# Delta rule: products of constants, read by nobody, at the places in levels three to five of the inverse where TensorE waits

## The reference, cut to what matters

```python
def gated_delta_chunked(q, k, v, log_a, beta, s0):
    ...
    g = jnp.cumsum(log_a, axis=-1)
    decay = jnp.exp(jnp.where(causal, g[..., :, None] - g[..., None, :], -jnp.inf))
    kk = jnp.einsum('bhncd,bhnsd->bhncs', k, k)
    lmat = jnp.where(strict, beta[..., :, None] * decay * kk, 0.0)
    rhs = jnp.concatenate([beta[..., None] * v, (beta * jnp.exp(g))[..., None] * k], axis=-1)
    sol = lax.linalg.triangular_solve(jnp.eye(GDN_CHUNK, dtype=f32) + lmat, rhs,
                                      left_side=True, lower=True, unit_diagonal=True)
    ...
    def step(s, inp):
        u0_c, w_c, aqk_c, qg_c, kg_c, gl_c = inp
        u = u0_c - w_c @ s
        o = qg_c @ s + aqk_c @ u
        s = gl_c[..., None, None] * s + jnp.swapaxes(kg_c, -1, -2) @ u
        return s, o
```

## Time and profile before

| what | value |
|---|---|
| median of 3 runs | 3951.13 us |
| the runs | 3950.55 to 3952.97 us |
| the profiled execution, its own time | 3950.24 us |
| its span, first to last instruction | 3948.4 us |
| outside the span | 1.8 us |
| mean granted TensorE clock | 0.994 of full speed |
| busy: PE, PEld, DVE, ACT, POOL | 97%, 73%, 56%, 19%, 18% |
| the delta rule's four heads | about 484 to 732 us |

### The profile page before, as it was taken

One profiled execution on the slowest core, in us unless ns is written; L12 is line 12 of the kernel. 1 busy time (PEld: TensorE's weight loads), 2 busy tenths in 40 slices (PEclk: granted clock), 3 DMA queues, 4 the chain that ended last, 5 costly groups with the idle time before them and its releaser, 6 DMA issues.

```text
span 3948.4 us, 48505 instructions
## 1 busy us (share of the span) xinstructions
PE 3838.0 (97%) x18602; PEld 2875.3 (73%) x18602; DVE 2228.2 (56%) x3856; ACT 742.5 (19%) x1402; POOL 721.9 (18%) x570
## 2 busy tenths in 40 slices
PE   7999988999999999999999999999999999999998
PEld 3455567565555556688888877888789898778886
DVE  4255676354446313326565765564788888556546
ACT  2144455221110013431100000000311111100002
POOL 0048853100000000000000002120244343121200
PEclk9999999999999999999999999999999999999999
DMA  5244400231211121112322322232222222122321
GB/s 192 89 167 149 139 2 1 71 90 53 63 53 59 59 75 43 33 60 80 85 83 88 85 77 92 87 102 86 77 70 70 70 73 64 54 85 85 101 86 64
DMA packets 381407, 312.13 MB, mean 79 GB/s; under 512 B 9552, under 2 KB 349904, under 8 KB 381136
## 3 DMA queue, kind: packets, MB, share of 16 engines
q1 hardware_dynamic: 381264, 310.16, 25.2%
HBM read 308.03 MB, written 2.10 MB: 79 GB/s over the span
## 4 chain that ended last, share of the span: by engine, by line
PE 87%; POOL 5%; DVE 3%; ACT 2%; issue 1%; DMA 1%; POOLq 0%; SPq 0%; DVEq 0%; ACTq 0%
PE ps_lin L967 18%; PE ps_lin L867 10%; PE ps_d L967 9%; PE ps_lin L1742 6%; PE ps_d L867 5%; PE ps_c L967 4%; PE ps_lin L750 4%; PE ps_lin L767 3%; PE ps_d L750 3%; PE ps_lin L813 3%; PE ps_lin L1158 3%; PE ps_c L867 3%; POOL arena L3506 2%; PE ps_d L1531 2%; POOL arena L3503 2%; PE ps_c L750 2%
## 5 line engine op out<-in xcount | busy, mean ns | idle before, releaser
L3475 POOL TENSOR_TENSOR rstd<-square 128x512 f32<-128x512 f32 (+2 forms) x12 | 15.1, 1260 | 1543.3 <-ACT square L1920 1543.3
L967 PE MATMUL ps_lin<-arena,ring 128*128 128x256 f32 (+1 forms) x800 | 217.2, 424 | 1.1 <-DVE arena L2597 1.1
L867 PE MATMUL ps_lin<-arena,ring 128*128 128x256 f32 (+1 forms) x864 | 214.1, 401 | 0.0
L967 PEld LDWEIGHTS ps_lin<-arena,ring 128*128 128x128 f32 x800 | 151.8, 190 | 60.9 <-issue 2.9
L867 PEld LDWEIGHTS ps_lin<-arena,ring 128*128 128x128 f32 x864 | 164.2, 190 | 41.1
L967 PE MATMUL ps_lin<-hid_in,arena 128*128 128x256 f32 x832 | 188.6, 380 | 3.6 <-DVE arena L2624 3.6
L3478 POOL TENSOR_TENSOR rstd<-rstd,square 128x512 f32<-128x512 f32 (+2 forms) x58 | 75.4, 1300 | 631.2 <-ACT square L1920 630.3
L967 PE MATMUL ps_d<-arena,mixed 128*128 128x384 f32 (+1 forms) x672 | 187.7, 432 | 0.0
L967 PE MATMUL ps_lin<-hid_in,mixed 128*128 128x384 f32 (+1 forms) x672 | 187.7, 432 | 0.0
L2621 DVE TENSOR_TENSOR arena<-ring 128x1024 f32<-128x1024 f32 x84 | 102.9, 1225 | 146.3 <-PE ps_d L867 136.0
L967 PEld LDWEIGHTS ps_lin<-hid_in,arena 128*128 128x128 f32 x832 | 157.7, 190 | 27.7 <-DVE arena L2624 5.6
(11 more groups left out here) (545 smaller groups left out, 8132.8 us busy)
## 6 DMA issues: line engine op xcount, KB each, us to landing
ring<-in_ffn_w_in SPq DMA_DIRECT2D x88, 512.0 KB, 4.6
resid<-in_ada_w SPq DMA_DIRECT2D x20, 2048.0 KB, 7.9
ring<-in_mlp_w_up SPq DMA_DIRECT2D x64, 512.0 KB, 4.5
ring<-in_mlp_w_down SPq DMA_DIRECT2D x64, 512.0 KB, 4.4
ring<-in_attn_w_qkv SPq DMA_DIRECT2D x64, 512.0 KB, 4.8
ring<-in_ffn_w_out SPq DMA_DIRECT2D x32, 512.0 KB, 4.1
ring<-in_even_w_in SPq DMA_DIRECT2D x28, 512.0 KB, 5.0
ring<-in_sc_w_in SPq DMA_DIRECT2D x24, 512.0 KB, 4.5
```

What stands on the lines that cost most here:

```text
L867: last = mm(prod[i - 1], lhs[:, j, :], rhs(p), start=(g == j == 0), stop=(g == G - 1 and j == np_ - 1))
L967: last = mm(out, lhs[:, j, :], rhs[:, j, :], start=(j == 0), stop=(j == 3))
```

## The change: what it does

A helper `keep_busy(count)` issues `count` matmuls of `ident` with the 256 columns of `upto` into columns 768 to 1023 of `ps_c`. They wait for no semaphore, release none, and nothing reads what they write. For heads 0 to 2 (n is not None) and levels 3, 4 and 5 they stand: in level 3, five ahead of the third group of products, two ahead of the third group of updates and seven behind it; in level 4, two ahead of the third group of updates; in level 5, seven behind the products and two ahead of the third group of updates. That is 25 matmuls a head, 75 in all. No other engine's instructions change.

```diff
+                def keep_busy(count):
+
+                    for _ in range(count):
+                        mm(psc[:, T:1024], ident, flat(m["upto"]), start=True, stop=True)
+
                 for e in range(1, LEVELS):
+                    busy = n is not None and 2 < e < LAST
                     if e == LAST:
...
                     for g in range(3):
+                        if busy and e == 3 and g == 2:
+                            keep_busy(5)
                         products(e, g)
+                    if busy and e == 5:
+                        keep_busy(7)
                     for g in range(3):
+                        if busy and g == 2:
+                            keep_busy(2)
                         updates(e, g)
+                    if busy and e == 3:
+                        keep_busy(7)
```

## The result

The kernel with the change takes 3958.08 us (median of 22 runs, 3956.02 to 3960.2), the one before 3950.37 us (22 runs, 3945.5 to 3952.97): 7.7 us more, a ratio of 1.0021 with a 95% interval of 1.0015 to 1.0027, which is 5.9 to 10.7 us. The profiled execution took 3958.11 us, its span is 3956.3 us.

The account below looks back on a forecast made before the run. TensorE, busy 97% of the span, was taken to bound the kernel: 16.2 us of added delay less 6.6 us from the clock gave +9.6 us on 3950.24 us, so 3959.9 us, with a range of 3952 to 3967 us.

Parts of the forecast that it names:

- The price of a matmul and of the turn: TensorE, heads 0 to 2: 0.429 us a new matmul, another 0.33 us for a group between quarter-array matmuls.
- Rival 1: Going between quarter and full array costs nothing: +4.6 us, 3954.8 us; chance 22%.
- The delays: Heads 0, 1 and 2, levels 3 to 5: added delay of 6.6, 4.8 and 4.8 us, together 16.2 us.
- The chain argument: Levels 3 to 5: each group less its idle time, remainders adding up on TensorE; 4.35 us at head 1's level 5 updates.
- One reading in the chain: Head 1, level 5: the transposes that ended the gap were taken to come 3.17 us late.
- What the clock gives back: Half-clock stretches avoided from level 5 on: 5.55 us in head 1, 1.00 us in head 2, together 6.6 us.
- The signs: Clock 1.00 from 505 to 720 us, 150 L1443 records, head 0's scan at 541.5 us, head 1's 64.8 us later.
- Rival 2: New matmuls don't hold the clock in these levels: +16.2 us at least, 3966.4 to 3970.3 us; chance 17%.
- The clock rule of the Trainium skill: Mid-kernel drops only behind pauses longer than any of levels 3 to 5; the change would be all cost, +16.2 us.
- Rival 3: Level 5 of each head: faster if avoided falls exceed 16.2 us; over 0.2% faster needs 24 us; chance 6%.
- Rival 4: Later stages shift against the clock's falls, up to 3.5 us either way, heads as forecast; chance 10%.

Follow-up runs that it names:

- the twos: The change without its nine groups of two matmuls ahead of third updates: 3953.91 us, ratio 1.0008 to the kernel before.
- level 5's groups: The change with its new matmuls in level 5 alone, 27 instead of 75: 3950.16 us, ratio 0.9997 to the kernel before.
- Levels 3 and 4 alone: The change with its new matmuls in levels 3 and 4 only, 48 of the 75: 3953.78 us, ratio 1.0008 to the kernel before.
- the cut groups: The change with groups cut to what the idle times hold, none ahead of third updates: 3943.09 us, ratio 0.9982 to the kernel before.
- the first set: First of two sets of four edited kernels, run on one chip beside the kernel before, whose median there was 3950.16 us (27 runs).
- the corner experiment: The change with all 75 matmuls on 32 x 32 of the array, same 256 columns: 3974.35 us, ratio 1.0055 to the kernel before.
- 11 matmuls: Half of the groups cut to the idle times, 11 matmuls in all instead of the change's 75: 3942.99 us, ratio 0.9984 to the kernel before.

## Why the prediction came out right

**The price of a matmul and of the turn.** Forecast 0.429 and 0.33 us. The columns are confirmed (0.216 us a record, two a matmul), and the way back to quarters measured 0.20 to 0.22 us behind groups of four, ten and fourteen records. The group of five, with both ways, delayed head 1 by 0.87 us where 0.86 was forecast. Rival 1, the free turn, falls: each group shows it.

**The delays.** 16.2 us forecast, 15.7 measured; half of the difference is head 0, 6.4 instead of 6.6. The chain argument, that each group is set against its own pause and the remainder adds up since TensorE decides from there, held in head 1 to 0.12 us in every row. The experiments with parts agree where the groups overflow their pauses: the twos 4.2 us on the medians and 4.8 in the traces against 4.0 to 4.5, level 5's groups 5.1 against 5.4. Levels 3 and 4 alone gave 8.9 against 10.8, because a pause left open behind them takes part of the delay back. One reading in the chain was off without harm: the transposes of level 5 are not 3.17 but 2.54 us late (they start 20.00 us after level 3's products instead of 17.46, in the change as with levels 3 and 4 alone), but with seven matmuls in front TensorE is later still.

**What the clock gives back.** 6.6 us forecast, from one profiled execution. In the two profiled executions it is just that: 15.7 us of delay, less 6.6, less 1.5 that the changed kernel's trace is ahead before level 3 of head 0, plus 0.2 behind the heads, is 7.8, and 7.9 lie between them. The 1.5 us were in no term of the sum, and since no instruction there differs they are chance: 1.1 us are there when head 0 starts, and 0.4 come with the fall near 495 us, which is 3.4 instead of 6.8 us long. Over the medians 15.7 - 7.7 = 8.0 us came back, with 5.0 to 9.8 from the interval of the result, and 7.1 us with the cut groups, with 3.6 to 11.1. So the runs can't tell 6.6 from 8.0, and the forecast of 3959.9 us, 1.8 over the median, is as near as they can show.

The size of this term was still luck, since it was read off a single draw. The executions beside the first set show how wide the draw is: 3945.35 us with a mean granted clock of 0.995, 3956.84 us with 0.992. That the one profiled before the change, 3950.24 us, lay next to the median could not be known from three runs. The prediction also gave 51% to a time over 3959.0 us, and the median is 0.9 us under it.

**The signs.** The start of head 0's scan was forecast at 541.5 us and came at 539.81, 1.7 us early, mostly the same 1.5 us. From there to head 1's scan it is 64.7 us (64.8 forecast), the 150 records of L1443 are there, and the clock is at full speed from 505 to 720 us.

**Rival 2** was wrong for this change, but its mechanism is real: the corner experiment has nearly the same delays, a busy TensorE, and falls. **The clock rule of the Trainium skill** (TensorE: Matmul & The Clock Gate, Why this matters for your kernels), by which pauses as short as these are harmless, does not describe levels 3 to 5. Work in the pauses, none over 1.95 us, took the falls away and was worth 7.1 us.

**Rival 3** failed on the cost side. The gain that it wanted from avoided falls exists, at 7 to 8 us, but the change pays 15.7 us for what 11 matmuls get for nothing in their traces. **Rival 4**: from L1233 at the end of the heads (729.87 and 737.52) to the end of the span the two traces differ by 0.2 us, so the later stages moved by nothing that counts here.

## What to carry to other kernels

Matmuls on the whole array that nobody reads can keep TensorE's clock up across pauses, but price each group against its own pause: columns, plus the turn to another tile size, against the idle time in the trace. Put in less than the pause holds, since half of it did as much here as the whole, and everything beyond is paid in full on a chain that TensorE decides. What clock falls cost should come from many runs or from a kernel without them, never from one profile.

## What the runs showed of the hardware that was not expected

- Busy is not what holds the clock. 75 matmuls of 256 columns on 128 x 128 of the array held it; on 32 x 32, at the same 0.22 us a record, it fell to half after 10 us in which TensorE had not been idle, and the kernel took 16 us more than with the full-array matmuls.
- A long pause isn't needed either. In one trace the clock fell for 6.8 us in head 3 with no pause over 0.57 us in the 24 us ahead.
- Falls differ in length and so in price: 3.4 us at half clock cost 1.0 to 1.6 us, 6.8 us in head 3 cost 3.0, 13.6 us cost 5.6 us in head 1.
- The 64 x 64 groups behind a full-array matmul start 0.2 us later than its columns need, whether 4, 10 or 14 records stand ahead. Behind ten or four 32 x 32 records it is 0.1 us.
